# A third of the first layer's conditioning: loaded in the prologue, or behind the blocks of the output projection

## What is computed

```python
mod = einsum('bd,lde->lbe', silu(c), ada_w) + ada_b      # ada_w: (4, 1024, 6144)
for l in range(4):
    sh_m, sc_m, gt_m, sh_f, sc_f, gt_f = split(mod[l], 6)
    u = rmsnorm(h, norm_g[l, 0]) * (1 + sc_m) + sh_m
    out = mixer(u)                                       # layer 0: (b_gate * conv3(c_gate * xi)) @ w_out
    h = h + gt_m * rmsnorm(out, norm_g[l, 1])
    u = rmsnorm(h, norm_g[l, 2]) * (1 + sc_f) + sh_f
    out = conv_ffn(u)
    h = h + gt_f * rmsnorm(out, norm_g[l, 3])
```

## Time and profile before

| | |
|---|---|
| median of 3 runs | 3015.58 us (3015.1 to 3020.77) |
| span of the profiled execution | 3014.3 us |
| TensorE busy | 2876.1 us, 95% |
| TensorE's mean granted clock | 0.979 of full speed |
| weight loads on TensorE (PEld) | 2733.3 us, 91% |
| VectorE, ScalarE, GpSimd busy | 51%, 36%, 44% |
| moved by DMA | 332.56 MB, mean 110 GB/s |
| first matmul of the first layer | at 53.24 us |
| output projection of the first layer | about 210.5 to 256.8 us |

### The profile page before, as it was taken

The page is one execution under the profiler, slowest core; times in us unless marked ns, Lnnn a source line. Parts: engine busy times, 40 slices in busy tenths (PEclk is TensorE's granted clock), DMA queues, the critical chain, the costliest instruction groups (busy, mean ns, idle before and its releaser), DMA issues.

```text
span 3014.3 us, 72962 instructions
## 1 busy us (share of the span) xinstructions
PE 2876.1 (95%) x29617; PEld 2733.3 (91%) x29617; DVE 1528.4 (51%) x2080; ACT 1085.0 (36%) x2139; POOL 1321.5 (44%) x959
## 2 busy tenths in 40 slices
PE   6999999998989999999998999999999999899998
PEld 5998999997978877899997899889999899799998
DVE  3435666118357874666603242476650444566612
ACT  4224333225455652433323444343332422433322
POOL 3443444442435554344443273434444344344443
PEclk9999999999999999999999999999999999899999
DMA  7544333544411013333354323533334543133332
GB/s 269 164 151 159 95 92 88 158 128 136 119 44 32 4 37 124 120 89 92 99 159 152 99 64 112 169 123 89 92 116 146 173 120 91 57 92 92 91 91 85
DMA packets 465618, 332.56 MB, mean 110 GB/s; under 512 B 19914, under 2 KB 435608, under 8 KB 465122
## 3 DMA queue, kind: packets, MB, share of 16 engines
q1 hardware_dynamic: 461400, 325.24, 35.1%
q10 hardware_dynamic: 4010, 4.22, 0.6%
HBM read 319.62 MB, written 10.20 MB: 109 GB/s over the span
## 4 chain that ended last, share of the span: by engine, by line
PE 62%; DVE 4%; ACT 2%; issue 1%; DMA 1%; SPq 0%; POOL 0%; ACTq 0%; DVEq 0%
PE banks L1667 33%; PE banks L1675 16%; PE banks L2126 5%; PE banks L2133 1%; PE banks L1628 1%; PE banks L1973 1%; DVE h L2662 1%; PE banks L1690 1%; DVE proj L2606 1%; PE banks L1761 0%; DMA s_state<-in_state_wkv_b_dram 0%; ACT conv L1080 0%; PE banks L2135 0%; ACT uv L1433 0%; DVE proj_b L2606 0%
## 5 line engine op out<-in xcount | busy, mean ns | idle before, releaser
L765 POOL TENSOR_TENSOR w_lo<-w_raw,w_hi 128x1024 fp32r<-128x1024 f32 x395 | 1007.5, 2551 | 1108.1 <-ACT w_hi L981 1088.0
L1667 PE MATMUL banks<-u_hi,w_hi 128*128 128x260 f32 x4064 | 834.5, 287 | 14.2 <-ACT w_hi L981 9.4
L1667 PE MATMUL banks<-u_lo,w_hi 128*128 128x260 f32 x4064 | 825.1, 284 | 0.0
L1667 PEld LDWEIGHTS banks<-u_hi,w_hi 128*128 128x128 f32 x4064 | 627.4, 189 | 27.1 <-issue 15.2
L1667 PEld LDWEIGHTS banks<-u_lo,w_hi 128*128 128x128 f32 x4064 | 629.9, 189 | 1.6
L981 ACT ACTIVATE w_hi<-w_raw 128x1024 fp32r<-128x1024 f32 x402 | 424.5, 1056 | 454.2 <-PE banks L1675 284.4
L1675 PE MATMUL banks<-u_hi,w_lo 128*128 128x260 f32 x4064 | 527.5, 282 | 0.0
L1675 PEld LDWEIGHTS banks<-u_hi,w_lo 128*128 128x128 f32 x4064 | 502.1, 187 | 1.3
L1667 PE MATMUL banks<-hid_hi,w_hi 128*128 128x260 f32 x1664 | 336.3, 283 | 0.0
L1667 PE MATMUL banks<-hid_lo,w_hi 128*128 128x260 f32 x1664 | 335.2, 283 | 0.0
L3113 DVE TENSOR_TENSOR csb<-proj 128x520 f32 (+1 forms) x42 | 30.3, 722 | 470.8 <-ACT proj L1048 470.8
(11 more groups left out here) (463 smaller groups left out, 3898.8 us busy)
## 6 DMA issues: line engine op xcount, KB each, us to landing
w_raw<-in_ffn_w_up_dram SPq DMA_DIRECT2D x176, 512.0 KB, 3.7
ada_raw<-in_ada_w_dram SPq DMA_DIRECT2D x96, 512.0 KB, 4.7
w_raw<-in_ffn_w_down_dram SPq DMA_DIRECT2D x64, 448.0 KB, 3.7
w_raw<-in_sconv_w_in_dram SPq DMA_DIRECT2D x48, 512.0 KB, 5.2
ada_ahead<-in_ada_w_dram SPq DMA_DIRECT2D x36, 512.0 KB, 7.7
ada_ahead_down<-in_ada_w_dram SPq DMA_DIRECT2D x36, 512.0 KB, 6.2
w_raw<-in_ffn_w_down_dram SPq DMA_DIRECT2D x32, 512.0 KB, 4.0
ada_pro<-in_ada_w_dram SPq DMA_DIRECT2D x6, 2048.0 KB, 21.2
```

Source lines behind the costliest of these rows:

```text
L765: pool.tensor_tensor(w_lo[:, s, :, :], w_raw[:, s, :, :], w_hi[:, s, :, :].bitcast(F32), ALU.subtract).then_inc(lo_done, 1)
L1667: pe.matmul(tile_ps[slot][half][0:width, 0:HALF], w_hi[:, s, k, 0:width], x[:, k0 + k, half * HALF:(half + 1) * HALF], start=start and k = ...
```

## The change

The prologue makes only shift and scale: four steps instead of six. The gate's eight columns are loaded by SyncE as four pairs into `ada_raw`, behind the weight blocks 0 to 3 of the first layer's output projection, and TensorE multiplies them two at a time behind blocks 1 to 4. ScalarE copies the sums behind block 5, TensorE turns them behind block 6, and VectorE adds the bias and multiplies by the gain (`first_gate`). `ada_used` starts at 18 instead of 26, and the waits on it, on `mod_mm` and on `acc_copied` are shifted to match. Five semaphores of small loads become one, with the counts at which each load has landed.

```diff
+PRO_STEPS = 2 * KT // PRO_T
...
+        FIRST_GATE = KT // 2
...
-                    sp.wait_ge(ada_used, a + 1 if h == 1 or pair > 7 else a - 5)
+                    sp.wait_ge(ada_used, a + 1 - KT if h == 1 else a + 1 if pair > 7 else a - 5)
...
+            def load_first_gate(x):
+
+                for s in range(2):
+                    i = 2 * x + s
+                    sp.wait_ge(ada_used, 2 + 2 * KT + GT + i - 1)
+                    sp.dma_start(ada_raw[:, s, :], ada_columns(0, 2 * KT + i)).then_inc(ada_loaded[s], 16)
...
-            for i in range(GT // PRO_T):
-                if i == len(ada_pro):
-                    sp.wait_ge(pro_mod_mm, 1)
+            for i in range(PRO_STEPS):
...
                         load_block(n0 + b, b % 2, w[:, :, b * P:(b + 1) * P])
+                        if l == 0 and b < FIRST_GATE:
+                            load_first_gate(b)
                         if b == 4 and in_norms(h):
...
+            def copy_first_gate():
+
+                act.wait_ge(ada_used, 2 + GT + KT * ADA_G)
+                act.wait_ge(mod_mm, 2 * KT + GT)
                 act.activation(acc_sb[:, :], acc_ps[:, 0:2 * P], ACT.Copy).then_inc(acc_copied, 1)
...
                         out_pair(it, False)
+                    if l == 0:
+                        copy_first_gate()
                     out_pair(p["iters"] - 1, True)
...
-            pe.sem_inc(ada_used, 2 + GT)
+            pe.sem_inc(ada_used, 2 + 2 * KT)
...
                 if i == 0:
                     pe.wait_ge(mod_ready, h)
+                    pe.wait_ge(first_gate_done, 1)
...
+                    elif l == 0:
+                        for b in range(2 * p["iters"]):
+                            out_block(b // 2, b % 2)
+                            if 1 <= b <= FIRST_GATE:
+                                for s in range(2):
+                                    pe.wait_ge(ada_loaded[s], 16 * (GT // 2 + b - 1) + 16)
+                                    if b == 1 and s == 0:
+                                        pe.wait_ge(mod_ready, 2)
+                                    ada_columns(ada_raw[:, s, :], 2 * (b - 1) + s)
+                            if b == 2 * p["iters"] - 2:
+                                turn_sums(-1, 0)
...
+            def first_modulation():
+
+                dve.wait_ge(mod_mm, 2 * KT)
+                bias = vecs[:, col["ada_b"]:col["ada_b"] + 2 * KT].unsqueeze(2).to_broadcast([P, 2 * KT, NSEQ])
+                gain = vecs[:, col["norm_g"]:col["norm_g"] + KT].unsqueeze(2).to_broadcast([P, KT, NSEQ])
+                scale = mod_m[:, KT:2 * KT, :]
+                link(dve.tensor_tensor(mod_m[:, 0:2 * KT, :], ada_ps[:, 0:2 * KT * NSEQ].rearrange("p (t s) -> p t s", s=NSEQ),
+                                       bias, ALU.add))
+                link(dve.tensor_scalar(scale, scale, 1.0, None, ALU.add))
+                dve.tensor_tensor(scale, scale, gain, ALU.mult).then_inc(mod_ready, 1)
+                dve.wait_ge(mod_ready, 1)
+
+            def first_gate():
+
+                dve.wait_ge(mod_mm, 2 * GT)
...
+                link(dve.tensor_tensor(gate_rows, ada_ps[:, 0:KT * NSEQ].rearrange("p (t s) -> p t s", s=NSEQ), bias,
+                                       ALU.add))
+                dve.tensor_tensor(gate_rows, gate_rows, gain, ALU.mult).then_inc(first_gate_done, 1)
```

More of the change, by code:

```diff
@@ L278, in trunk_kernel @@
         pro_mod_mm, pro_mod_copied = sem("pro_mod_mm"), sem("pro_mod_copied")
-        ada_pro_loaded = [sem(f"ada_pro_loaded{i}") for i in range(GT // PRO_T)]
+        ada_pro_loaded = [sem(f"ada_pro_loaded{i}") for i in range(6)]
+        first_gate_done = sem("first_gate_done")
         ada_used = sem("ada_used")
@@ L472, in pair_of @@
             return pair if pair < GT // 2 else None
+        FIRST_GATE = KT // 2
         def raw_turn(h, pair):
-            return pair if h == 1 else GT // 2 + (h - 2) * 6 + {3: 0, 7: 1}.get(pair, pair - 6)
+            return pair if h == 1 else GT // 2 + FIRST_GATE + (h - 2) * 6 + {3: 0, 7: 1}.get(pair, pair - 6)
         def ahead_of(h):
@@ L1025, in copy_sums @@
             def copy_sums(group):
-                act.wait_ge(ada_used, 2 + GT + KT * (group + 1))
-                act.wait_ge(mod_mm, GT + KT * group)
+                late = 0 if group >= ADA_G else KT
+                act.wait_ge(ada_used, 2 + GT + KT * (group + 1) - late)
+                act.wait_ge(mod_mm, GT + KT * group - late)
+                act.activation(acc_sb[:, :], acc_ps[:, 0:2 * P], ACT.Copy).then_inc(acc_copied, 1)
+            def copy_first_gate():
+                act.wait_ge(ada_used, 2 + GT + KT * ADA_G)
+                act.wait_ge(mod_mm, 2 * KT + GT)
                 act.activation(acc_sb[:, :], acc_ps[:, 0:2 * P], ACT.Copy).then_inc(acc_copied, 1)
@@ L1612, in _ @@
                 pe.sem_inc(s, 2)
-            pe.sem_inc(ada_used, 2 + GT)
+            pe.sem_inc(ada_used, 2 + 2 * KT)
             row_groups = ident[:, :].rearrange("p (g c) -> p g c", g=NG)[:, :, 0:NSEQ]
             def turn_sums(group, first_tile):
-                pe.wait_ge(acc_copied, group + 1)
+                late = group < ADA_G
+                pe.wait_ge(acc_copied, group + (1 if late else 2) if group >= 0 else ADA_G + 1)
                 for i in range(2):
@@ L1655, in ada_ahead @@
                 else:
-                    pe.wait_ge(ada_pro_loaded[i % KT], 16 * (2 * (h - 2) + i // KT + 2))
+                    pe.wait_ge(ada_pro_loaded[i % KT], 16 * (2 * (h - 2) + i // KT + (2 if i % KT < PRO_STEPS else 1)))
                     ada_columns(ahead_of(h)[i % KT][:, :], i % KT)
@@ L1762, in spread_rstd @@
                 mm.then_inc(rstd_turned, 1)
-            for i in range(GT // PRO_T + 1):
+            for i in range(PRO_STEPS + 1):
                 if i == VEC_STEP:
@@ L2530, in modulation @@
                 g = 2 * l + half
-                dve.wait_ge(mod_mm, GT * (g + 1))
+                dve.wait_ge(mod_mm, GT * (g + 1) - (KT if g == 1 else 0))
                 if True:
@@ L2569, in _ @@
                     link(dve.tensor_copy(vecs[:, 512:nrow], bank[3][:, 0:nrow - 512]))
-            modulation(0, 0, mod_m)
+            def first_modulation():
[10 more added lines that the diff above has]
+                dve.wait_ge(mod_mm, 2 * GT)
+                c0 = col["ada_b"] + 2 * KT
+                bias = vecs[:, c0:c0 + KT].unsqueeze(2).to_broadcast([P, KT, NSEQ])
+                c0 = col["norm_g"] + KT
+                gain = vecs[:, c0:c0 + KT].unsqueeze(2).to_broadcast([P, KT, NSEQ])
+                gate_rows = mod_m[:, 2 * KT:3 * KT, :]
+                link(dve.tensor_tensor(gate_rows, ada_ps[:, 0:KT * NSEQ].rearrange("p (t s) -> p t s", s=NSEQ), bias,
+                                       ALU.add))
+                dve.tensor_tensor(gate_rows, gate_rows, gain, ALU.mult).then_inc(first_gate_done, 1)
+                dve.wait_ge(first_gate_done, 1)
+            first_modulation()
             def conv3(q, e, name, row0, m, ft):
@@ L3139, in _ @@
                     dve.tensor_tensor(csb[:, 0, :], csb[:, 0, :], csb[:, 1, :], ALU.add).then_inc(sum_ready, 1)
+                    if p["kind"] == "out" and l == 0:
+                        first_gate()
                     if p["kind"] == "down" and l + 1 < depth:
```

38 lines of the change are left out of this document (19 added, 19 removed).

## The result

The changed kernel takes 3062.13 us (median of 4 runs, 3059.55 to 3062.61), against 3017.87 for the kernel before (4 runs, 3015.1 to 3020.77): a ratio of 1.0143, with a 95% interval from 1.0128 to 1.0157. It is slower by 44 us. The profiled execution took 3062.57 us, with a span of 3060.8; the one of before had 3014.3.

The account below looks back on a forecast made before the run. TensorE, busy 95% of the span, was taken as the bound, so time is lost where it waits or works longer. -9.7 + 0.8 + 26.4 + 16.2 + 0.6 + 6.4 = +40.7 us gave 3056 us, range 3040 to 3070.

Parts of the forecast that it names:

- Gain of the prologue: Prologue's serial tail: two of six steps removed, so the layer's first matmul starts 9.7 us earlier, bounds 8.5 to 10.5.
- Weight block 1: Output projection, first gate load: weight block 1 stands behind it, its high part 0.8 us late, from 0 to 3.
- Three short waits: Output projection: weight blocks 2, 3 and 4 issued only after the block before ends; 8.8 us each, 26.4 in all.
- Long wait: Behind block 4 of the output projection: a conditioning pair and six loads precede weight block 5; 16.2 us, 14 to 18.2.
- Turn: Turn of the gate's sums on TensorE in the output projection: costs 0.6 us.
- Clock behind the four waits: TensorE's blocks behind the four new waits restart at half clock: 1.6 us lost each, 6.4 in all, 0 to 12.

Follow-up runs that it names:

- The warm start: The weights first, plus nine unread matmuls in TensorE's idle stretch before the layer's first block; ratio 0.9963 to the kernel before, 3011.4 us.
- The weights first: Changed kernel with only SyncE's load order altered: gate pairs behind weight blocks 1, 3, 4, 5, loads for half 2 behind block 7; ratio 0.9976 to before, 3012.09 us.
- the short waits alone: Changed kernel with gate loads as changed, but the pair and six loads ahead for half 2 behind weight block 7; ratio 1.0066 to the kernel before.
- the added matmuls: Changed kernel with unread matmuls behind the gate columns, 14 behind blocks 1, 2 and 3, 34 behind block 4; ratio 1.0115 to the kernel before.
- the small loads: Changed kernel with each of the eight gate loads bringing 64 KB instead of 512 KB; ratio 1.0108 to the kernel before.

## Why the prediction was right, point by point

3056 was forecast and 3062 measured, inside the range, for the reason given. The sum forecast 40.7 us up to the mark, where 43.3 were found; the 2.6 between are nearly all in the clock's term, and the other misses cancel. By its own terms:

- Gain of the prologue: 9.7 forecast, 10.4 found. VectorE's tail was a little shorter than worked out, and the weights came early enough (35.38, as forecast). The seven others with this prologue found 9.4 to 11.5, so the 0.7 above the forecast is within the scatter.
- The first pair of blocks took 14.4 us instead of 13.3, since the clock stayed at half until about 48.9: +1.1, a term that the sum hadn't. The warm start shows that the clock is its cause, but it is no cost of the change: six of the other seven executions with the changed prologue took 13.5 us or less.
- Weight block 1: 0.8 forecast, 0.56 of idle time found.
- Three short waits: 26.4 forecast, 25.8 found (8.5 + 8.8 + 8.5). The weights first and the short waits alone show that the place of the load in the queue is their cause.
- Long wait: 16.2 forecast, 16.5 found.
- Turn: 0.6 forecast, 0.5 found.
- Clock behind the four waits: 6.4 forecast. The blocks behind them took 7.8, 8.0, 8.3 and 7.8 us (the last: 280.15 to 287.94, where the next begins) against 5.74, so 9.0 together. This is the mis-sized term. Some 0.6 of it is not the clock, since such a block took 5.8 to 5.9 us at full clock when the added matmuls filled the wait; the clock is 8.4, or 2.1 a wait instead of 1.6. That the stand was longer than the 2 us of the earlier trace rows is not shown to be the reason: behind 7 us and behind 15 the loss is the same here, and with the small loads, behind 5.8 to 6.0 us, the blocks took 8.3, 7.5 and 7.2.

Sum -10.4 + 1.1 + 0.6 + 25.8 + 16.5 + 0.5 + 9.0 = 43.1; the mark says 43.3. The prediction also says that the loads ran at 395 GB/s at best; over 1180:1190 of that trace 402 GB/s moved, which changes no term. The rest of the 46.5 us between the two spans lies in the RWKV stage, from the root at 689.51 to the one at 1214.37 and their like: 524.9 us before and 528.7 after, which is more than that rest. I had said that both traces should run alike from there on, and here they don't. But the other kernels, which are the same in that stage, have 528.0, 527.9, 527.8, 521.2, 528.9, 527.7, 524.7 and 524.1 (in the order told here), and the kernel before itself ran between 3009 and 3026 us over all chips. So the stage scatters by some 7 us from execution to execution, and this is no part of the change that I can show; the medians of the runs differ by 44.3 us, near the 43.3 of the mark. Most of the scatter lies in its last part, behind the root of the group norm (1138.47 before, 1181.22 after): 75.9 us before, 80.1 after, 73.8 to 79.5 in the others. In that part TensorE waits for VectorE's gated rows for 5.1 us after the change, and not at all in the kernel before and in the two executions with 73.8. Why it does in some executions stays open, and whether a shifted start moves the stage's mean was not settled.

## What to carry to other kernels

A load that has to wait for its buffer is a wait for every load behind it in the issuing queue; put it behind those that are due sooner, and count at what moment each place in the queue is reached, not only whether the bytes fit. Here the same loads in another order made 48 us up to the first norm (some 1 us of it scatter of the first matmul), with all other instructions the same. Such a wait costs more than its idle time, since TensorE restarts at half its clock; and a load moved from a saturated stretch into one bound by TensorE gives back only the difference (10.4 us less 4.8 for the columns and 0.5 for the turn).

## What I had not expected of the hardware

- Behind a stand of 7 to 15 us TensorE ran its next block at half clock for 4 to 5 us and lost 1.9 to 2.4 us; unread matmuls in the stand removed that (5.8 to 5.9 us a block). How long the half clock lasts scatters: 3.4 to 6.2 us at the layer's first blocks, in nine executions. The Trainium skill, TensorE: Matmul & The Clock Gate, section HAM oscillation, describes a cost of this kind, paid again behind every wait for data; this trace agrees, for all four waits.
- Landing times scatter even on an idle queue: 6.6 to 6.9 us for three loads of 512 KB in the changed kernel, once 9.6 in the same place of another, 1.0 of it spent on the issue.
- The same stage of the same code took from 521.2 to 528.9 us in ten profiled executions.
